# Index-query and latent weights in two depth halves: the start of a decoder layer on one Trainium2 core

## The reference, cut to what matters

```python
h = rms_norm(x, norm_mix[l])
z = h @ w_in[l]
oa = moba_attention(qa, ka, va, bias_a) @ w_oa[l]       # qa, ka, va, qb, ckv, q_idx, k_idx, w_idx,
ckv = rms_norm(z[..., OFF_CKV:OFF_IQ], ckv_norm[l])     # ga, gb are column ranges of z
q_idx = z[..., OFF_IQ:OFF_IK]                           # 256 columns, right behind ckv's 256
k_idx = z[..., OFF_IK:OFF_IW]
ob = dsa_attention(qb, kb, vb, q_idx, k_idx, w_idx, bias_b) @ w_ob[l]
x = x + (ga * oa + gb * ob) @ w_out[l]
x = x + memory_cross_attention(rms_norm(x, norm_x[l]), rms_norm(mem, mem_norm[l]), ...)
x = x + hier_moe(rms_norm(x, norm_moe[l]), ...)         # 32 experts, all their weights are read
```

## Time and profile before

| | |
|---|---|
| median of 3 runs | 675.29 us (675.01 to 675.73) |
| span of the profiled execution, first to last instruction | 674.2 us |
| median less that span | 1.1 us |
| TensorE busy | 507.5 us, 75% of the span |
| DMA moved | 244.21 MB, 362 GB/s on average |
| VectorE, ScalarE busy | 204.2 us, 145.2 us |
| granted TensorE clock, mean | 0.885 of full speed |

### The profile page before, as it was taken

The page is one execution under the profiler, slowest core; times in us unless marked ns, Lnnn a source line. Parts: engine busy times, 40 slices in busy tenths (PEclk is TensorE's granted clock), DMA queues, the critical chain, the costliest instruction groups (busy, mean ns, idle before and its releaser), DMA issues.

```text
span 674.2 us, 8772 instructions
## 1 busy us (share of the span) xinstructions
PE 507.5 (75%) x3803; PEld 321.7 (48%) x3803; DVE 204.2 (30%) x376; ACT 145.2 (22%) x252; POOL 16.2 (2%) x31
## 2 busy tenths in 40 slices
PE   8999999999999997967644845763474677438475
PEld 7999998999999742412311411231141123114121
DVE  4798665588857431100000100000010000001002
ACT  5764545354545511000000000000000000000002
POOL 1200010001001000000000000000000000000001
PEclk9999999999999988997956988796697778579889
DMA  9899433608899999999999999999999999999993
GB/s 292 257 333 371 173 125 125 250 1 307 301 387 385 417 372 431 428 428 428 429 427 428 427 429 428 428 428 427 430 427 430 424 431 426 430 425 430 424 409 146
DMA packets 49113, 244.21 MB, mean 362 GB/s; under 512 B 9064, under 2 KB 18736, under 8 KB 37296
## 3 DMA queue, kind: packets, MB, share of 16 engines
q1 hardware_dynamic: 49072, 243.62, 89.4%
HBM read 242.53 MB, written 4.22 MB: 366 GB/s over the span
## 4 chain that ended last, share of the span: by engine, by line
PE 52%; DMA 43%; SPq 2%; DVE 1%; ACT 1%; issue 1%; POOL 0%; POOLq 0%
PE ps L711 16%; DMA slots_late<-in_w 13%; PE ps L1073 11%; DMA slots_own<-in_w 9%; DMA attn_data<-in_w 7%; PE ps L734 7%; PE ps L1078 6%; DMA slot_last<-in_w 4%; DMA slot_mixed<-in_w 4%; DMA slot_spare<-in_w 3%; SPq L544 1%; PE ps L689 1%; DMA slots_own<-in_w_in 1%; PE ps L833 1%; PE ps L862 1%; PE ps L1183 1%
## 5 line engine op out<-in xcount | busy, mean ns | idle before, releaser
L1073 PE MATMUL ps<-slots_late,x_sb 128*32 128x512 f32 x320 | 86.3, 689 | 39.3 <-DMA slots_late<-in_w 16.2
L1073 PE MATMUL ps<-slot_spare,x_sb 128*32 128x512 f32 x128 | 59.4, 663 | 14.3 <-DMA attn_data<-in_w 14.3
L1810 DVE TENSOR_TENSOR slot_extra<-ps,slot_extra 128x512 f32<-128x512 f32 x8 | 5.5, 692 | 212.2 <-ACT slot_extra L1437 212.2
L1073 PE MATMUL ps<-attn_data,x_sb 128*32 128x512 f32 x160 | 61.3, 698 | 10.7 <-DMA slots_own<-in_w 10.7
L435 DVE TENSOR_TENSOR w_low<-slots_own,w_high 128x2048 fp32r<-128x2048 f32 (+1 forms) x32 | 64.7, 2022 | 15.2 <-ACT w_high L1247 14.9
L1434 ACT ACTIVATE slot_extra<-ps 128x256 f32<-128x256 f32 x8 | 3.1, 384 | 299.9 <-PE ps L1141 299.9
L1078 PE MATMUL ps<-slots_own,slot_extra 128*32 128x512 f32 x192 | 49.5, 719 | 16.5 <-DMA slots_late<-in_w 8.8
L1073 PE MATMUL ps<-slots_own,x_sb 128*32 128x512 f32 x240 | 53.3, 630 | 9.3 <-DMA slot_last<-in_w 3.4
L1078 PE MATMUL ps<-attn_data,slot_extra 128*32 128x512 f32 x112 | 46.3, 746 | 16.7 <-DMA slots_own<-in_w 16.7
L1247 ACT ACTIVATE w_high<-slots_own 128x2048 fp32r<-128x2048 f32 (+1 forms) x32 | 54.2, 1696 | 20.2 <-PE ps L734 10.8
L711 PE MATMUL ps<-h_high,w_high 128*128 128x256 f32 x224 | 55.4, 288 | 0.0
(11 more groups left out here) (258 smaller groups left out, 866.8 us busy)
## 6 DMA issues: line engine op xcount, KB each, us to landing
slots_own<-in_w SPq DMA_DIRECT2D x27, 2048.0 KB, 33.4
slots_late<-in_w SPq DMA_DIRECT2D x23, 2048.0 KB, 34.8
attn_data<-in_w SPq DMA_DIRECT2D x16, 2048.0 KB, 33.9
slot_last<-in_w SPq DMA_DIRECT2D x9, 2048.0 KB, 36.4
slots_own<-in_w_in SPq DMA_DIRECT2D x8, 2048.0 KB, 12.4
slot_spare<-in_w SPq DMA_DIRECT2D x8, 2048.0 KB, 35.6
slot_mixed<-in_w SPq DMA_DIRECT2D x7, 2048.0 KB, 35.5
slots_own<-in_w_out SPq DMA_DIRECT2D x2, 2048.0 KB, 8.7
```

What stands on the lines that cost most here:

```text
L1073: return pe.matmul(ps[SLOTS * e:SLOTS * e + SLOTS, 4 + matrix, :], xeT[:, k, SLOTS * e:SLOTS * e + SLOTS], w, start=(k == 0), stop=(k == K ...
L1810: dve.tensor_tensor(act_sb, ps[:, 5, :].rearrange("p (q f) -> p f q", f=FC), silu_sb.rearrange("p (f q) -> p f q", f=FC), ALU.mult).then_i ...
```

## The change

The two sets of weights, `ckv` (columns 2048 to 2303) and `iq` (columns 2304 to 2559), lie side by side in memory, and are now loaded together: two transfers of 1 MB, each with half the depth (four blocks) of all 512 columns, in runs of 2 KB. Both are issued where `iq`'s transfer stood, ahead of `ikw` and the tables. The conversions and the products of `iq` go by the same halves. ScalarE makes `h_high` of blocks 4 to 7 between the two halves of `w_high`. VectorE takes the scaling of token tile 1.

```diff
             if name in ("iq", "ckv"):
-                return "ckv_iq", halves("ckv_iq")[:, ("iq", "ckv").index(name)]
+                at = 256 * ("ckv", "iq").index(name)
+                return "ckv_iq", w512("ckv_iq")[:, :, at:at + 256]
...
-            elif name == "iq":
+            elif name == "ckv":
                 eng.wait_ge(iq_in, 16)
+                chunk_landed(eng, "ckv_iq")
...
-            sp.dma_start(halves("ckv_iq")[:, 0], cols(C_IQ, 256)).then_inc(iq_in, 16)
+            for i, signal in enumerate((iq_in, slot_in[0])):
+                sp.dma_start(w512("ckv_iq")[:, 4 * i:4 * i + 4, :], cols(C_CKV, 512)[:, 4 * i:4 * i + 4, :]).then_inc(signal, 16)
             sp.dma_start(w_ikw, cols(C_IK, IDX_DIM + IDX_HEADS)).then_inc(ikw_in, 16)
             sp.dma_start(rel_sb[:], rel_bias).then_inc(tab_in, 16)
             sp.dma_start(one_hot, buckets).then_inc(tab_in, 16)
             sp.dma_start(below_sb, below).then_inc(tab_in, 16)
-            sp.dma_start(halves("ckv_iq")[:, 1], cols(C_CKV, 256)).then_inc(slot_in[0], 16)
...
+            pe.wait_ge(iq_high_set, 1)
+            index_queries(wh, h_high, range(4), first=True)
+            pe.wait_ge(iq_low_set, 1)
+            index_queries(wl, h_high, range(4))
+            pe.wait_ge(iq_high_set, 2)
+            index_queries(wh, h_high, range(4, KD))
+            index_queries(wh, h_low, range(4))
+            pe.wait_ge(iq_low_set, 2)
+            index_queries(wl, h_high, range(4, KD))
+            m = index_queries(wh, h_low, range(4, KD), last=True)
...
-            act.wait_ge(rstd_set[1], 1)
-            act.activation(xn[:, 1, :], x_sb[:, 1, :], ACT.Copy, scale=rstd[:, 0, 1:2]).then_inc(xn_set[1], 1)
-            split_weights(0)
+            def split_iq(i):
+
+                ks = slice(4 * i, 4 * i + 4)
+                if i:
+                    chunk_landed(act, "ckv_iq")
+                else:
+                    act.wait_ge(iq_in, 16)
+                act.activation(part(w_high, "iq")[:, ks], weights("iq")[1][:, ks], ACT.Copy).then_inc(iq_high_set, 1)
+
+            split_iq(0)
             act.wait_ge(gain0_set, 1)
             for b in range(2, 4):
                 split_turned(0, b, 0, h_high)
+            split_iq(1)
+            act.sem_inc(split_high, 1)
             split_weights(1)
...
+            dve.wait_ge(rstd_set[1], 1)
+            dve.tensor_scalar(xn[:, 1, :], x_sb[:, 1, :], rstd[:, 0, 1:2], None, ALU.mult).then_inc(xn_set[1], 1)
...
-            low_weights(dve, SPLITS[0])
-            for b in range(4):
+            def low_iq(i):
+
+                ks = slice(4 * i, 4 * i + 4)
+                dve.wait_ge(iq_high_set, i + 1)
+                dve.tensor_tensor(part(w_low, "iq")[:, ks], weights("iq")[1][:, ks], part(w_high, "iq")[:, ks].bitcast(F32),
+                                  ALU.subtract).then_inc(iq_low_set, 1)
+
+            low_iq(0)
+            for b in range(2):
+                split_turned(0, b, 0, h_high, h_low)
+            low_iq(1)
+            dve.sem_inc(low_set[0], 1)
+            for b in range(2, 4):
                 split_turned(0, b, 0, h_high, h_low)
```

More of the change, by code:

```diff
@@ L297, in decoder_layer @@
         mem_in, ident_in, const_in, gain_in = sem("mem_in"), sem("ident_in"), sem("const_in"), sem("gain_in")
-        iq_in = sem("iq_in")
+        iq_in, iq_high_set, iq_low_set = sem("iq_in"), sem("iq_high_set"), sem("iq_low_set")
         x_in = [sem(f"x_in{t}") for t in range(TT)]
@@ L756, in _, with index_queries @@
             wh, wl = part(w_high, "iq"), part(w_low, "iq")
[L757 to L762, removed]
+            def index_queries(w, x_, ks, first=False, last=False):
+                for k in ks:
+                    if k % 2 == 0 and x_ is h_low:
+                        pe.wait_ge(h_low_set, k // 2 + 1)
+                    elif k % 2 == 0 and w is wh:
                         pe.wait_ge((h_first_set, h_high_set)[k // 4], k // 2 % 2 + 1)
-                    if k % 2 == 0 and j == 2:
-                        pe.wait_ge(h_low_set, k // 2 + 1)
                     for i in range(2):
                         m = pe.matmul(o[:, i * T:(i + 1) * T], w[:, k, i * P:i * P + P], x_[:, k, :],
-                                      start=(i + k + j == 0), stop=(k == KD - 1 and j == 2), skip_group_check=True)
+                                      start=(first and i + k == 0), stop=(last and k == KD - 1), skip_group_check=True)
+                return m
+            pe.wait_ge(iq_high_set, 1)
[8 more added lines that the diff above has]
+            m = index_queries(wh, h_low, range(4, KD), last=True)
             end(m, "iq")
```

## The result

The changed kernel took 681.29 us (median of 6 runs, 678.20 to 682.78) against 675.51 us before (6 runs, 675.01 to 675.99): the ratio is 1.0077, with a 95% interval from 1.0062 to 1.0093. The forecast was 678.4 us, 676.0 to 679.5. The change made the kernel slower, as forecast, by the mechanism that was forecast, but by 5.8 us where 2.9 were expected over the old median. The measured median lies above the range. The profiled execution of the changed kernel took 680.05 us, with a span of 678.3.

A forecast was written before the change was run, and what follows sets the result against it. The prediction took TensorE's front to bound the kernel: +1.6 us for late tables and +1.5 for a halved clock made +3.1, so span 674.2 became 677.3, plus 1.1 around it 678.4 us, range 676.0 to 679.5.

The forecast's parts named there:

- What bounds the kernel, and that the front carries over: TensorE's front, up to about 240 us, sets the expert stream; a microsecond won or lost there reaches the end whole.
- The order of the transfers decides: ckv's 1 MB now precedes the tables, which TensorE awaits before all of iq; ikw starts at 20.2, +1.6 us.
- Rival C: Front: tables not late, landing at 11.27 us as before, so the kernel is 0.6 us faster, 674.7 us; chance 0.11.
- Rival D: Front: no change, tables at 11.7 to 12.5 us because fewer runs could free SyncE sooner; chance 0.06.
- Rival A: Front: tables late but TensorE's clock stays, +1.6 us (1.3 to 2.1), 676.9 us; chance 0.30.
- The tables at 13.5: Tables land at 13.5 us, taken between 13.2 and 13.97, against 11.27 before; iq then begins at 14.37.
- Estimate (b): Tables' landing: the old 11.27 us plus 1.05 MB at 389 GB/s, 2.70 us, gives 13.97 us.
- Estimate (a): Tables' landing: 13.83 us for the same set before, less 0.66 us lost during SyncE's hold, gives 13.2 us.
- What the wait covers: In the front, iq's inputs are ready ahead of use; VectorE's 0.7 us gain is covered by the tables' wait, worth nothing.
- The clock: TensorE idles 3.0 us before iq, so its clock likely halves for 3.41 us, costing 1.5 us in iq and ikw.
- The sum: Whole kernel: +1.6 us for late tables and +1.5 for the slow clock, +3.1 (2.3 to 3.8), 678.4 us; chance 0.48.
- Scaling and halves: VectorE's front: scaling tile 1 gains 0.3 us; with the halves its chain ends at 17.9 instead of 18.56 us.

The follow-up runs named there:

- experiment 7: Changed kernel with the tables issued first, but only iq's 1 MB in two halves with 1 KB runs, ckv one transfer behind ikw: 674.69 us, ratio 0.9985.
- experiments 2 and 4: Changed kernel with the table product moved behind the iq products, ratio 0.9993; changed kernel with 17 more filler products ahead of the tables' wait, ratio 1.0027.
- Experiments 1, 2 and 3: Changed kernel with tables issued first, 0.9978; changed kernel with table product behind iq, 0.9993; kernel before with only ckv's transfer moved ahead of ikw and tables, 1.0072.

## Why the prediction was right or wrong

**What bounds the kernel, and that the front carries over: right.** Over the thirteen profiled executions whose own time is known, the time less the start of `ikw` lies between 655.9 and 657.7 us, while the start itself moves from 17.3 to 24.0. The carry is whole within about 1 us. Up to the first expert product it is closer than that: from `ikw` to that product it is 221.3 to 221.6 us in ten of the fourteen profiles, among them all three of the changed kernel. Behind it the executions differ by up to 1.4 us, whatever their front did.

Three of the other four are the two profiles of the kernel before (221.8 and 222.8 us) and the one with the scaling alone (221.8). In these the clock stood at half for some 3.4 us between 236 and 241 us. The rows of the kernel before show no pause ahead of it, but TensorE busy throughout, at the end with 24 narrow products (36 columns):

```profile
232.76:236.17 3.41, 3.41 (x34) 3.41 (x33) 1.55 (x5) 2.73 (x3) 0.91 (x3) 1.00 1.03 416
236.17:239.58 3.41, 3.41 (x6) 1.36 (x6) 2.44 (x19) 2.60 (x4) 0.00 (x0) 0.50 1.01 423
```

No other kernel shows such a stretch there (the fourth profile over 221.6 is that of experiment 7, 222.1, cause open). It makes the kernel before 0.5 and 1.4 us slower in its two profiles than its front alone would. That may be why experiments 2 and 4, set against it, lost some 1.2 and 0.8 us less than their `ikw` came later. With two profiles of the kernel before, that is not shown for its median.

**The order of the transfers decides: right.** Experiments 1, 2 and 3 show it from three sides. **Rival C (the tables are not late): out;** they landed behind both halves in every profile with that order. Its sum (-0.6 to -0.7) comes near to what the kernel with the tables first does in the front (17.81 less 18.60 is -0.8). **Rival D (SyncE freed sooner by fewer runs): out;** SyncE was held longer, not shorter. **Rival A (late tables, clock stays): out** in all three profiles.

**The tables at 13.5: the first step that failed.** They let the product start at 14.93 (14.36 and 14.71 in the other two profiles). Estimate (b) priced 1 MB at the 389 GB/s of a later stretch. The rate of this very stretch is lower, before and after the change:

```profile
5.00:14.00 9.00, 7.16 (x52) 5.72 (x51) 4.46 (x7) 6.67 (x11) 1.71 (x4) 1.00 1.02 318
```

```profile
5.00:14.00 9.00, 5.55 (x39) 5.05 (x37) 5.59 (x12) 4.55 (x10) 1.76 (x4) 0.98 1.03 324
```

With it (b) gives 11.27 + 1.05 / 0.32 = 14.6. Estimate (a) took 0.66 us away for a gap of low rate that it laid to SyncE's hold. A low rate came back in the changed kernel, 281 GB/s at 12 to 14 us, with the DMA engines busy (share 0.99). Without that subtraction (a) gives 13.8, still 1.1 us short of 14.93, and what makes up that part is not shown. The term was 2.23 us and measured 3.66.

**What the wait covers: right.** All inputs of `iq` were there ahead of use, VectorE's gain was covered, and `iq` and the table product together took 6.60 us at full clock, against 0.87 + 5.85 = 6.72 forecast.

**The clock: right in kind, the second step that failed in size.** That the pause would bring the clock down was forecast with odds of about 8 to 5, and it did in all three profiles. One stretch of 3.41 us and 1.5 us of cost were taken; two of three executions had 6.83 us, and the cost in the first profile was 2.46. The pause was longer than forecast (4.38, not 3.0), but that one error fed the other is not shown: 6.83 us of slow clock came with a pause of 3.70, and 3.41 us with one of 4.39.

**The sum.** The front moved by 3.66 - 0.73 + 2.46 = 5.39 us in the profiled execution, where 2.23 - 0.61 + 1.5 = 3.1 was forecast. Its span grew by 4.1 us: 1.3 us of the front's loss are not in it, of which 0.5 is the old profile's slow stretch near 238 us, and 0.8 comes behind the first expert product, cause open. The time around the span was 1.75 us where the prediction took 1.1, a figure it got by setting a profiled execution's span against the median of others. Together 680.05 against 678.4: 1.0 us by the span and 0.65 by the time around the span. The median of the runs lies another 1.2 us higher, by the unprofiled group above 682, and that part of the miss is unexplained.

**2 KB runs: counted at zero,** and nothing else was shown. **Scaling and halves:** the scaling alone is not told apart from nothing. The halves were not run alone. With the tables first both of them and the order together give 1.4 us, of which the order alone gave 0.8; the best kernel of the study is that one, at 674.15 us against 675.57.

## What to carry to other kernels

When a transfer is moved forward in a queue, go down the list of everything it passes, and ask of each small one who waits for it and what stands behind that waiter: here 74 KB of tables with one cheap product held 48 others. Price the bytes that are put ahead at the rate of that very stretch, not at the best rate of the trace. And when TensorE is made to wait for a few microseconds, ask what a slow clock behind the pause would add to the price. In this kernel it cost 1.5 to 2.5 us in the profiled executions. The medians of the kernels with and without fillers differ by 3.0 and 4.3 us.

## What the runs showed of the hardware

- Transfers of the same order and size let the table product start 1.4 us apart in two executions (12.69 and 14.07), with 367 and 298 GB/s at 5 to 8 us.
- The clock did not fall over a pause of 2.46 us once, and fell over 3.70, 3.85, 4.38 and 4.39 us. The slow stretches were 3.41 or 6.83 us long, the longer ones not behind the longer pauses, and could begin before TensorE had its next work (at 13.67 with the product at 14.93).
- The clock also fell for some 3.4 us without a pause, near 236 us in the kernel before, behind a stretch in which TensorE was busy 3.41 of 3.41 us. The same 24 products ran at 238.92 in the changed kernel with no fall behind them.
- With a fixed program the times of the changed kernel spread over 4.6 us (678.20 to 682.78), of the one with the tables first over 1.2 us (673.72 to 674.90). That the pause makes it so is not shown: the kernel with the scaling alone, which has no such pause, spread over 3.5 us (674.96 to 678.47).
